# Bias rows of a routed expert layer, made in the routing stage of one core's kernel

## The chip, the cores and the metric

The kernel runs on one core of one Trainium2 chip as a single program. The metric is device time in microseconds (us), taken as the median of several executions; lower is better. Engines are called PE (TensorE), DVE (VectorE), ACT (ScalarE), POOL (GpSimd) and SP (SyncE, which here only starts transfers).

## The reference

One layer of an encoder with 16 meta tokens and 1024 tokens of width 1024, all in fp32. What matters here is what follows attention:

```python
mixed = jnp.concatenate([out_a, out_b], axis=-1)
h = h + mixed @ w_out[l]
v = _rmsnorm(h, g_ffn[l]).reshape(B * L, D_MODEL)
y = _moe(v, ...)          # logits = v @ w_router + b_router; top 4 of 32 experts; gates = softmax(top 4)
h = h + y.reshape(B, L, D_MODEL)
...
def expert_block(args):
    xb, e = args
    a = xb @ w_mlp1[e] + b_mlp1[e]
    return _clamped_swiglu(a) @ w_mlp2[e] + b_mlp2[e]
ys = ys * slot_gate[:, None].astype(ys.dtype)
return jax.ops.segment_sum(ys, slot_tok, num_segments=T + 1)[:T]
```

The part with `b_mlp2` can be split off: for each token it is the sum over its four experts of gate times `b_mlp2[e]`, that is one row of `gates (1024 x 32) @ b_mlp2 (32 x 1024)`. These are the "bias rows".

## The kernel before, in words

**Stages.** Five stages follow one another: `project`, `attend_window`, `attend_diff`, `route`, `experts`. Each is a block: every engine has its own instruction list, engines wait for one another only through semaphores, and a block ends when all five have arrived. An engine's list is worked through strictly in order, so an instruction that waits holds up all behind it on its engine. The change touches `route` and `experts` only.

**fp32 products.** A product is made of fp32r parts: a "high" copy (ACT) and a "low" remainder (DVE: value minus high), and three matmuls, high x high, high x low, low x high.

**`route`** handles eight tiles of 128 tokens (`NT` = 8), in a software pipeline. In PE's iteration t it does: `project_out(t, 0)` (24 matmuls of 512 columns), `transpose_mixed(t + 1)`, `ranks(t - 2)`, `transpose_v(t - 1, 0)`, half of `project_out(t, 1)`, `transpose_v(t - 1, 1)`, the other half, `logits(t - 1)`. DVE's iteration t does: `residual(t, 0)`, `copy_mt(t + 1)` (the low parts of the turned tile), `place(t - 2)` (gates, slot numbers, and a dense row of gates per token, L1359), `heads(t + 2)`, `residual(t, 1)`, `normalise(t)`, in iteration 4 the low part of `b_mlp2` (L1383), `choose(t - 1)` (top 4, ends with `sel`, L1342). ACT makes high parts, squares, roots and exponents. SP stores each tile of h (`sums`, the output tensor) and of v (`v_dram`). POOL scatters each token's number and gate to its four slots in `slot_dram` (L1223, an indirect DMA per pick) and at the stage's end waits until all 32 scatters have landed. After the last tile DVE and PE make the list of jobs (L1387 to L1416): a job is up to 256 slots of one expert; the kinds are "one" (up to 128), "few" (up to 192) and "two".

**`experts`** first sets up, then runs a loop over the jobs. Setting up before the change:

- SP reads the first job's slots (`idn`, L1621), then starts loading weights; each weight piece is 1 MB, twelve to a job, and four pieces of the first expert were loaded during `route`.
- POOL clears `xg`, gathers the first job's rows of v (L1652), spreads `b_mlp1` over the partitions (L1667), and adds the bias rows to the output tensor by eight accumulating DMAs (L1670).
- PE turns the dense gates (L2111), makes the bias rows in eight steps of two matmuls (L2119), each step waiting until ACT or DVE has emptied the bank of the step before last, then turns the first job's rows (`transpose_x0(0)`, L1996), waits for the last copies and enters the job loop.
- ACT makes the high part of the gates (L1819), the high parts of weight pieces 0 to 2 (L1732), four copies of bias rows (L1824), `keep_x0(0)` (L1757), and enters the loop.
- DVE makes the low part of the gates (L1973), the low parts of pieces 0 to 2 (L1845), four copies (L1979), `keep_x0(0)` (L1904), waits until the first three accumulating DMAs have landed, and enters the loop.

In the loop PE's first product needs the low part of the first rows (`x0_lo`) and of piece 0; piece k + 3 is split in step k of the loop.

Of the kernel before, what the change touches and what calls it, by code (L numbers as in the profile page):

```python
# [26 lines left out]
P = 128  # L27
D = 1024
# [512 lines left out]
class BiasRows:  # L541
# [3 lines left out]
    HIGH, LOW = slice(N_EXP, 2 * N_EXP), slice(2 * N_EXP, 3 * N_EXP)  # L545

    def __init__(self, nc, ctx):
        sb = lambda n, s, d=F32: ctx.enter_context(nc.sbuf_tensor(n, s, d))
        self.ident = sb("ident5", [P, P])
        self.dense = sb("dense_gates", [P, NT, 3, N_EXP])  # L550
        self.b2_p = sb("b2_parts", [3 * N_EXP, D], F32R)
# [560 lines left out]
def route(nc, a, mixed, gates, picks, jobs, bias, sums, v_dram, slot_dram, weights):  # L1112


    with ExitStack() as ctx:
# [13 lines left out]
        h2 = sb("h2", [P, 2, D])  # L1129
# [21 lines left out]
        b2 = sb("b2", [3 * N_EXP, D])  # L1151
        share = sb("share", [P, TOP_K, N_EXP])
# [4 lines left out]
        h2_sem = [sem(f"h2_stored{i}") for i in range(2)]  # L1157
# [12 lines left out]
        b2_landed, b2_high = sem("b2_landed"), sem("b2_high")  # L1170
# [10 lines left out]
        turned = lambda: tm_ps[:, :, :].rearrange("p b (c n) -> p (b c) n", n=P)  # L1181

        @block.sync
        def _(sp):
# [8 lines left out]
            sp.dma_start(bias.ident[:, :], a["consts"][:, C_ID:C_ID + P]).then_inc(b2_landed, 16)  # L1193
            for t in range(NT):
                sp.wait_ge(h2_done, 2 * (t + 1))
                sp.dma_start(sums[t * P:(t + 1) * P, :], h2[:, t % 2, :]).then_inc(h2_sem[t % 2], 16)
# [8 lines left out]
            for i in range(2):  # L1205
                sp.wait_ge(h2_sem[i], 16 * (NT // 2))
                sp.wait_ge(v_sem[i], 16 * (NT // 2))

        @block.gpsimd
        def _(pool):  # L1210

            pool.memset(none[:, :, 1], 0).then_inc(ready, 1)
# [13 lines left out]
            pool.wait_ge(scattered, 16 * NT * TOP_K)  # L1226

        @block.scalar
        def _(act):
# [15 lines left out]

            act.wait_ge(landed, 16 * NL)
# [7 lines left out]
            for t in range(NT + 1):  # L1254
                if t + 1 < NT:
                    copy_mt(t + 1)
                if t >= 1:
                    u = t - 1
                    for b in range(2):
                        act.wait_ge(tv_ready, 2 * u + b + 1)  # L1260
                        if b == 0 and u >= 1:
                            act.wait_ge(r_ready, u)
                        act.copy(vt[:, 4 * b:4 * b + 4, :], tv_ps[:, :].rearrange("p (c n) -> p c n", n=P)).then_inc(vt_done, 1)
                if t + 2 < NT:
                    head_std(t + 2)
                if t < NT:
# [4 lines left out]
                    act.activation(vs[:, t % 2, :], h2[:, t % 2, :], ACT.Square, accum_out=ss[:, t:t + 1]).then_inc(ss_done, 1)  # L1271
                    act.wait_ge(ss_done, t + 1)
                    act.activation(rs[:, t:t + 1], ss[:, t:t + 1], ACT.Sqrt, bias=eps[:, 0:1], scale=1.0 / D).then_inc(std_done, 1)
                if t == 3:
                    act.wait_ge(b2_landed, 64)
                    act.copy(bias.b2_p[:, :], b2[:, :]).then_inc(b2_high, 1)
                if t >= 1:
# [5 lines left out]
        def _(dve):  # L1283
# [31 lines left out]
            def residual(t, b):  # L1315
                dve.wait_ge(x_sem[t % 2], 16 * (t // 2 + 1))
                if t >= 2:
                    dve.wait_ge(v_done, t - 1)
                    dve.wait_ge(h2_sem[t % 2], 16 * (t // 2))
                dve.wait_ge(o_ready, 2 * t + b + 1)  # L1320
                dve.tensor_tensor(h2[:, t % 2, 512 * b:512 * b + 512], o_ps[:, 2 * (t % 2) + b, :],
                                  xs[:, t % 2, 512 * b:512 * b + 512], ALU.add).then_inc(h2_done, 1)

            def normalise(t):
                dve.wait_ge(std_done, t + 1)
                step(dve.reciprocal(rs[:, t:t + 1], rs[:, t:t + 1]))
                dve.scalar_tensor_tensor(out=vs[:, t % 2, :], in0=h2[:, t % 2, :], scalar=rs[:, t:t + 1], in1=gf[:, :],
# [16 lines left out]
            def place(u):  # L1344
# [7 lines left out]
                for k in range(TOP_K):  # L1352
# [6 lines left out]
                step(dve.tensor_reduce(bias.dense[:, u, :, :], share[:, :, :].rearrange("p k e -> p e k").unsqueeze(1)  # L1359
                                       .broadcast_to((P, 3, N_EXP, TOP_K)), AX.X, ALU.add))  # L1360
# [8 lines left out]
            for t in range(NT + 2):  # L1369
                if t < NT:  # L1370
                    residual(t, 0)
                if t + 1 < NT:
                    copy_mt(t + 1)
                if t >= 2:
# [6 lines left out]
                if t == 4:  # L1381
# [827 lines left out]
```

## Time and profile before

| | us |
|---|---|
| median of 3 runs | 2428.54 (2428.15 to 2431.27) |
| the profiled execution's own time | 2426.24 |
| its span, first to last instruction | 2424.6 |
| of it, `route` | 726.2 to 890.0 |
| first matmul of the job loop | 916.8 |
| last matmul of the job loop | 2408.0 |
| PE busy, share of the span | 2281.5 (94%) |

All times of rows are from the profiled execution, from the start of its span. The mean granted clock of PE over it is 0.971 of full speed. A row of the timeline has start, duration, engine, line, operation and tiles; in brackets stand the idle time before it and what ended it.

### The profile page before, as it was taken

How to read it: one execution, taken by the hardware profiler on the slowest of the kernel's cores; microseconds unless marked ns; L12 is line 12 of the kernel's file. 1: busy time of each engine (PE TensorE's matmuls, PEld its weight loads, DVE VectorE, ACT ScalarE, POOL GpSimd, SP SyncE). 2: the span in 40 equal slices, each digit the busy share in tenths (PEclk: the TensorE clock that was granted, in tenths of full speed). 3: DMA queues.
4: the chain of work that ended last, by engine and by line, in shares of the span. 5: the costliest groups of instructions: out<-in, count | busy, mean ns of one | idle time of the engine just before them, and what ended most of it. 6: DMA issues, size and time to landing. Idle time of an engine off the chain costs nothing. (4 is left out here: it accounts for less than half of the span.)

```text
span 2424.6 us, 34957 instructions
## 1 busy us (share of the span) xinstructions
PE 2281.5 (94%) x10657; PEld 1715.7 (71%) x10658; DVE 1874.5 (77%) x2403; ACT 1399.9 (58%) x1672; POOL 593.9 (24%) x555
## 2 busy tenths in 40 slices
PE   6999699999998948999999999999999999999996
PEld 5778565555546836777777877777777777777875
DVE  4476455999966757889897589788888878989986
ACT  4322354888864436666675457565656555757755
POOL 0133000111110233324142113231133221423523
PEclk9999799899998958999999999999999999999999
DMA  5243730333105639889797669796889777979986
GB/s 161 64 122 97 154 65 22 99 71 70 36 1 158 106 123 317 319 285 341 268 371 243 200 234 362 275 319 224 268 288 313 241 236 245 370 245 364 376 293 225
DMA packets 251919, 519.68 MB, mean 214 GB/s; under 512 B 28657, under 2 KB 60657, under 8 KB 251809
## 3 DMA queue, kind: packets, MB, share of 16 engines
q1 hardware_dynamic: 229666, 480.01, 58.8%
q0 software_dynamic: 22176, 38.70, 7.0%
q8 instruction: 42, 0.69, 0.1%
q14 instruction: 35, 0.29, 0.0%
HBM read 493.06 MB, written 60.15 MB: 228 GB/s over the span
## 5 line engine op out<-in xcount | busy, mean ns | idle before, releaser
L1845 DVE TENSOR_TENSOR wlo<-raw_first,whi 128x2048 fp32r<-128x2048 f32 x259 | 618.6, 2406 | 115.4 <-ACT whi L1732 103.2
L1732 ACT CAST whi<-raw_first 128x2048 fp32r<-128x2048 f32 x259 | 489.3, 1907 | 144.4 <-PE gl_ps L2024 95.0
L2026 PE MATMUL gl_ps<-whi,xt_hi 128*128 128x512 f32 x1056 | 418.6, 396 | 16.2 <-DVE wlo L1845 7.8
L2028 PE MATMUL gl_ps<-whi,xt_lo 128*128 128x512 f32 x1056 | 412.4, 391 | 0.0
L2027 PE MATMUL gl_ps<-wlo,xt_hi 128*128 128x512 f32 x1056 | 412.2, 390 | 0.0
L1845 DVE TENSOR_TENSOR wlo<-raw_later,whi 128x2048 fp32r<-128x2048 f32 x128 | 292.1, 2282 | 57.2 <-ACT whi L1732 57.2
L1732 ACT CAST whi<-raw_later 128x2048 fp32r<-128x2048 f32 x128 | 240.9, 1908 | 65.7 <-PE gl_ps L2024 48.0
L2026 PEld LDWEIGHTS gl_ps<-whi,xt_hi 128*128 128x128 f32 x1056 | 198.7, 188 | 69.3 <-issue 11.9
L2028 PEld LDWEIGHTS gl_ps<-whi,xt_lo 128*128 128x128 f32 x1056 | 198.8, 188 | 42.9
L2027 PEld LDWEIGHTS gl_ps<-wlo,xt_hi 128*128 128x128 f32 x1056 | 199.0, 188 | 40.0
L1652 POOL DMA_INDIRECT xg<-v_dram,idn x67 | 123.4, 1841 | 402.6 <-PE t_ps L1996 318.4
L2026 PE MATMUL y_ps<-whi,ht_hi 128*128 128x512 f32 x512 | 206.5, 403 | 0.0
L2028 PE MATMUL y_ps<-whi,ht_lo 128*128 128x512 f32 x512 | 200.0, 391 | 0.0
L2027 PE MATMUL y_ps<-wlo,ht_hi 128*128 128x512 f32 x512 | 199.5, 390 | 0.0
L757 DVE CUSTOM_DVE_ANT_0 e<-s_ps,zero,meta_nm 128x1024 f32<-128x1024 f32 x128 | 163.5, 1278 | 11.7 <-DVE dsb L772 9.6
L2024 PE MATMUL gl_ps<-wlo,xt_hi 128*64 128x512 f32 x416 | 164.7, 396 | 0.0
L2023 PE MATMUL gl_ps<-whi,xt_hi 128*128 128x512 f32 x416 | 162.3, 390 | 0.0
L1705 POOL DMA_INDIRECT out_h<-ys,idc x64 | 126.8, 1981 | 122.1 <-ACT ys L1776 76.7
L685 ACT ACTIVATE e<-e,nm 128x1040 f32<-128x1040 f32 x128 | 149.1, 1165 | 9.5 <-DVE nm L757 8.4
L870 PE MATMUL o_ps<-pt,v_all 128*64 128x512 f32 (+1 forms) x288 | 139.0, 605 | 0.0
L484 PE MATMUL pp<-w_in_hi,ut_hi 128*128 128x512 f32 (+3 forms) x344 | 132.0, 384 | 2.4 <-DVE ut_lo L345 2.4
L1701 POOL PARTITION_BROADCAST b<-b x32 | 91.9, 2873 | 166.7 <-DMA b<-in_b_mlp 163.6
(282 smaller groups left out, 4045.4 us busy)
## 6 DMA issues: line engine op xcount, KB each, us to landing
raw_first<-in_w_mlp SPq DMA_DIRECT2D x260, 1024.0 KB
raw_later<-in_w_mlp SPq DMA_DIRECT2D x130, 1024.0 KB
k_st<-qk_dram SPq DMA_DIRECT2D x32, 260.0 KB, 7.4
xs<-in_x SPq DMA_DIRECT2D x16, 512.0 KB, 3.9
w_in_raw<-in_w_in SPq DMA_DIRECT2D x32, 256.0 KB
q_st<-qk_dram SPq DMA_DIRECT2D x32, 256.0 KB, 6.6
qk_dram<-qk_hi SPq DMA_DIRECT2D x24, 256.0 KB, 2.4
qk_dram<-qk_lo SPq DMA_DIRECT2D x24, 256.0 KB, 2.8
```

The source lines that it names most:

```text
L484: pe.matmul(out, ut_hi[:, k, cols(i)], whi[:, s, 0:w], start=(k == 0), stop=False)
L685: act.activation(e[:, n % 2, i, :], e[:, n % 2, i, :], ACT.Exp, bias=nm[:, k:k + 1], scale=-1.0, accum_out=total[:, n % 16, i:i + 1]).then ...
L757: dve.tensor_tensor_reduce(e[:, n % 2, i, 0:SEQ], S(i), zero[:, :], -1.0, meta_nm[:, (n // NT) % 2, at:at + 1], ALU.add, ALU.min, nm[:, k: ...
L870: ins = pe.matmul(o_ps[DV:P, :], vt, pt[0:r, g % 2, c, :], start=(c == 0), stop=(c == 8), skip_group_check=True)
L1705: pool.indirect_dma_start(out=sums[:, :], out_offset=bass.IndirectOffsetOnAxis(ap=idc[:, half, 0:1], axis=0), in_=ys[:, half, :], in_offse ...
L1732: act.copy(whi[:, k % SPL, :], raw(k)).then_inc(hi_done, 1)
L1845: dve.tensor_tensor(wlo[:, k % SPL, :], raw(k), whi[:, k % SPL, :].bitcast(F32), ALU.subtract).then_inc(lo_done, 1)
L2023: ins = pe.matmul(bank, xh[:, 1, kc, :], hi, start=start, stop=stop, skip_group_check=True)
L2024: ins = pe.matmul(bank[0:FEW], xh[:, 1, kc, 0:FEW], lo, start=False, stop=stop, skip_group_check=True)
L2026: pe.matmul(bank, xh[:, half, kc, :], hi, start=start, stop=False, skip_group_check=True)
L2027: pe.matmul(bank, xh[:, half, kc, :], lo, start=False, stop=False, skip_group_check=True)
L2028: return pe.matmul(bank, xl[:, half, kc, :], hi, start=False, stop=stop, skip_group_check=True)
```

## The change

- `BiasRows` becomes `FirstRows`, which holds the buffers of the first job's rows (`xg`, `idn`), one more tile of sums (`last`) and three semaphores, so that they live through both stages.
- In `route`, h of tile t is kept in SBUF: in `mixed[:, t, :]`, whose attention output has been used by then, and for the last tile in `last`. DVE's `residual` no longer waits for earlier stores of h.
- Each tile's gates are turned on PE (`turn_gates`), split by ACT (`high_gates`) and DVE (`low_gates`), multiplied on PE (`bias_row`, two matmuls of 512 columns) into banks that the stage already has, and added by DVE (`add_row`) to the kept h. SP stores the sum only then (`store_sum`). The low part of `b_mlp2` is made in DVE's iteration 3, before 4.
- At the end of `route` SP waits for the scatters and reads the first job's slots, and POOL gathers the first job's rows there; POOL clears `xg` at the stage's start.
- On PE the last two calls, `turn_gates(NT - 1)` and `bias_row(NT - 1)`, stand among and behind the matmuls of the job list. From `experts` all work on bias rows is gone: the turning of the gates, eight products, eight copies, eight accumulating DMAs and the waits for them. POOL clears `ys` at its start.

```diff
 (DVE, place)
-                step(dve.tensor_reduce(bias.dense[:, u, :, :], ..., AX.X, ALU.add))
+                if u >= 2:
+                    dve.wait_ge(gt_ready, u - 1)
+                dve.tensor_reduce(dense[:, u % 2, :, :], ..., AX.X, ALU.add).then_inc(dense_done, 1)
+            def low_gates(u):
+                dve.wait_ge(gt_high, u + 1)
+                dve.tensor_tensor(gates_p[HIGH, u % 2, :], gt_ps[HIGH, :], gates_p[HIGH, u % 2, :].bitcast(F32), ALU.subtract
+                                  ).then_inc(gt_low, 1)
+            def add_row(u):
+                dve.wait_ge(row_ready, u + 1)
+                dve.wait_ge(v_done, u + 1)
+                dve.tensor_tensor(h2(u).rearrange("p (b n) -> p b n", n=512), row_bank(u),
+                                  h2(u).rearrange("p (b n) -> p b n", n=512), ALU.add).then_inc(row_added, 1)
...
             for t in range(NT + 2):
+                if 3 <= t <= NT:
+                    low_gates(t - 3)
+                if 4 <= t <= NT - 1:
+                    add_row(t - 4)
                 if t < NT:
                     residual(t, 0)
...
+                if t == NT + 1:
+                    low_gates(NT - 2)
                 if t >= 2:
                     place(t - 2)
...
                     residual(t, 1)
                     normalise(t)
-                if t == 4:
+                if t == 3:
                     dve.wait_ge(b2_high, 1)
+                    dve.tensor_tensor(b2_p[LOW], b2[LOW, :], b2_p[LOW].bitcast(F32), ALU.subtract).then_inc(b2_low, 1)
+                if t == NT:
+                    add_row(NT - 4)
+                    add_row(NT - 3)
                 if 1 <= t <= NT:
                     choose(t - 1)
 (DVE, behind the job list)
+            add_row(NT - 2)
+            add_row(NT - 1)
 (PE, transpose_mixed)
                 if t >= 1:
                     pe.wait_ge(mt_low, t)
+                if t >= 5:
+                    pe.wait_ge(row_added, t - 4)
 (PE)
+            def turn_gates(u):
+                pe.wait_ge(dense_done, u + 1)
+                pe.wait_ge(vt_done, 2 * min(u + 2, NT - 1))
+                if u >= 1:
+                    pe.wait_ge(gt_low, u)
+                pe.transpose(gt_ps, dense[:, u % 2, :, :].rearrange("p i e -> p (i e)"), ident).then_inc(gt_ready, 1)
+            def bias_row(u):
+                pe.wait_ge(gt_low, u + 1)
+                if u == 0:
+                    pe.wait_ge(b2_low, 1)
...
+                for c in range(2):
+                    ins = pe.matmul(row_bank(u)[:, c, :], gates_p[:, u % 2, :], b2_p[:, 512 * c:512 * c + 512], start=True, stop=True)
+                ins.then_inc(row_ready, 1)
...
+                project_out(t, 1, KC // 2, KC)
+                if t >= 3:
+                    bias_row(t - 3)
+                if t >= 1:
                     logits(t - 1)
+                if t >= 2:
+                    turn_gates(t - 2)
+            transpose_v(NT - 1, 0)
+            transpose_v(NT - 1, 1)
+            ranks(NT - 2)
+            bias_row(NT - 3)
+            logits(NT - 1)
+            turn_gates(NT - 2)
+            ranks(NT - 1)
+            bias_row(NT - 2)
...
 (SP)
+            def store_sum(u):
+                sp.wait_ge(row_added, u + 1)
+                sp.dma_start(sums[u * P:(u + 1) * P, :], h2(u)).then_inc(sums_stored if u < NT - 1 else rows1.last_stored, 16)
...
+            for u in range(NT - 4, NT - 1):
+                store_sum(u)
+            sp.wait_ge(scattered, 16 * NT * TOP_K)
+            sp.dma_start(rows1.idn[:, :, :], slot_dram[0:JOB, :]...).then_inc(idx_first, 16)
+            store_sum(NT - 1)
+            sp.wait_ge(sums_stored, 16 * (NT - 1))
 (POOL)
-            pool.wait_ge(scattered, 16 * NT * TOP_K)
+            for i in range(2):
+                pool.wait_ge(v_sem[i], 16 * (NT // 2))
+            pool.wait_ge(rows_set, 1)
+            pool.wait_ge(idx_first, 16)
+            for half in range(2):
+                pool.indirect_dma_start(out=rows1.xg[:, half, :], ..., in_=v_dram[:, :], ...).then_inc(rows1.x_landed[half], 16)
 (experts, PE)
-            for t in range(NT):
-                ins = pe.transpose(t_ps[...], bias.dense[:, t, :, :]..., ident[:, :])
-            ins.then_inc(gt_ready, 1)
-            pe.wait_ge(gt_low, 1)
-            for t in range(NT):
-                if t >= 2:
-                    pe.wait_ge(b_copied[t % 2], t // 2)
-                for c in range(2):
-                    ins = pe.matmul(bias_banks(t)[:, c, :], gates_p[:, t * P:(t + 1) * P], bias.b2_p[...], start=True, stop=True)
-                ins.then_inc(b_ready, 1)
             transpose_x0(0)
-            for half in range(2):
-                pe.wait_ge(b_copied[half], NT // 2)
 (experts, DVE)
-            for t in range(1, NT, 2):
-                dve.wait_ge(b_ready, t + 1)
-                dve.tensor_copy(stage[t], bias_banks(t)).then_inc(b_copied[1], 1)
             keep_x0(0)
-            dve.wait_ge(b_stored[0], 16 * 3)
```

## Rows read from the trace of the kernel before

**Rows 1.** The page, busy time of PE.
```profile
PE 2281.5 (94%) x10657; PEld 1715.7 (71%) x10658; DVE 1874.5 (77%) x2403; ACT 1399.9 (58%) x1672; POOL 593.9 (24%) x555
```
**Rows 2.** Windows: engines' busy time, then clock, DMA share, GB/s.
```profile
798.67:813.65 14.98, 14.98 (x87) 12.86 (x86) 11.56 (x38) 7.64 (x12) 4.19 (x4) 1.00 0.88 106
...
859.40:864.90 5.50, 0.01 (x1) 0.01 (x1) 3.36 (x14) 3.45 (x7) 0.00 (x0) 0.58 0.50 184
...
889.96:916.81 26.85, 12.29 (x32) 7.65 (x33) 14.04 (x9) 12.68 (x11) 13.38 (x12) 0.50 0.93 276
```
**Rows 3.** Timeline of PE in `route`, iterations 4 and 5.
```profile
804.25 1.03 PE L1429 MATMUL tm_ps<-cst,mixed 128*128 128x128 f32 x8
...
811.95 1.86 PE L1461 MATMUL r_ps<-w_router_sb,vt 128*128 128x32 f32 x16
...
821.36 0.41 PE L1467 MATMUL r_ps<-acc,ones 128*128 128x32 f32 x2 [1.10 <-DVE sel L1342]
```
**Rows 4.** Timeline of DVE in `route`, iterations 3 and 4.
```profile
801.64 1.28 DVE L1327 SCALAR_TENSOR_TENSOR vs<-h,rs,g_ffn_sb 128x1024 f32<-128x1024 f32 x1
...
806.37 1.22 DVE L1307 TENSOR_TENSOR mt_lo<-tm_ps,mt_hi 128x1024 fp32r<-128x1024 f32 x1 [0.81 <-ACT mt_hi L1240]
...
817.94 1.22 DVE L1383 TENSOR_TENSOR b_parts<-b,b_parts 32x1024 fp32r<-32x1024 f32 x1
...
820.93 0.37 DVE L1342 TENSOR_REDUCE sel<-chosen 128x32 f32<-128x128 f32 x1
```
**Rows 5.** Timeline of the end of `route`.
```profile
867.84 0.82 DVE L1359 TENSOR_REDUCE dense_gates<-share 128x96 f32<-128x384 f32 x1
...
869.38 3.62 PE L1461 MATMUL r_ps<-w_router_sb,vt 128*128 128x32 f32 x16 [0.68 <-ACT vt L1263]
...
873.12 0.19 DVE L1333 TENSOR_TENSOR lg<-r_ps,b_router_sb 128x32 f32<-128x32 f32 x1 [4.45 <-issue]
...
882.07 0.96 POOL L1223 DMA_INDIRECT slot_dram<-code,dsti  x1 [0.30 <-issue]
...
885.33 0.15 DVE L1416 CAST jobs<-r_ps 1x1 int32<-1x1 f32 x1
```
**Rows 6.** POOL's sequencer at the block's end: ns, start in us.
```profile
L1115 POOLq COMPARE_BRANCH  x1: 49/49/49, 886.8 to 886.8; - x1
L1115 POOLq DRAIN  x1: 2758/2758/2758, 886.9 to 886.9; - x1
```
**Rows 7.** Timeline of the start of `experts`.
```profile
889.96 0.38 SPq L1621 DMA_DIRECT2D idn<-slot_dram  x1
...
892.81 1.06 POOL L1652 DMA_INDIRECT xg<-v_dram,idn  x1 [1.03 <-DMA idn<-slot_dram]
...
894.18 1.01 POOL L1652 DMA_INDIRECT xg<-v_dram,idn  x1 [0.30 <-issue]
...
895.54 6.70 DVE L1845 TENSOR_TENSOR wlo<-raw_first,whi 128x2048 fp32r<-128x2048 f32 x3 [0.58 <-ACT whi L1732]
...
904.05 2.30 POOL L1667 PARTITION_BROADCAST b<-b  x1 [8.86 <-issue]
...
912.64 1.23 DVE L1904 TENSOR_TENSOR xt_lo<-t_ps,xt_hi 128x1024 fp32r<-128x1024 f32 x1 [1.53 <-ACT xt_hi L1757]
...
916.81 0.79 PE L2026 MATMUL gl_ps<-whi,xt_hi 128*128 128x512 f32 x1 [5.26 <-PEq L2070]
```
**Rows 8.** DMA issues, 745 to 960: KB each, median us to landing.
```profile
out_h<-h SPq DMA_DIRECT2D x8, 512.0 KB, 5.1
...
xg<-v_dram,idn POOLq DMA_INDIRECT x5, 7.6
```
**Rows 9.** Timeline between the first job and the second.
```profile
957.50 0.49 PE L2026 MATMUL gl_ps<-whi,xt_hi 128*128 128x512 f32 x1 [3.63 <-DVE wlo L1845]
...
957.71 2.30 POOL L1701 PARTITION_BROADCAST b<-b  x1
...
957.88 4.13 DVE L1845 TENSOR_TENSOR wlo<-raw_first,whi 128x2048 fp32r<-128x2048 f32 x1 [1.12 <-ACT whi L1732]
```

More of the change, by code:

```diff
@@ L1108, in _, with route @@
                     act.copy(ot[:, u % 2, :], o_ps[0:DV, :]).then_inc(ot_done, 1)
-def route(nc, a, mixed, gates, picks, jobs, bias, sums, v_dram, slot_dram, weights):
+def route(nc, a, mixed, gates, picks, jobs, rows1, sums, v_dram, slot_dram, weights):
     with ExitStack() as ctx:
@@ L1128, in route @@
         mt_lo = sb("mt_lo", [P, 2, KC, P], F32R)
-        h2 = sb("h2", [P, 2, D])
         vs = sb("vs", [P, 2, D])
@@ L1253, in _ @@
             head_std(1)
-            for t in range(NT + 1):
+            for t in range(NT + 3):
+                if 3 <= t:
+                    high_gates(t - 3)
                 if t + 1 < NT:
                     copy_mt(t + 1)
-                if t >= 1:
+                if 1 <= t <= NT:
                     u = t - 1
@@ L1497, in _, with experts @@
             pe.matmul(r_ps[0:1, 128 + 2 * NJ:128 + 3 * NJ], ec[:, 2:3], ej[:, 2, :], start=True, stop=True).then_inc(cnt_ready, 1)
-def experts(nc, a, first, bias, jobs, v_dram, slot_dram, sums):
+            bias_row(NT - 1)
+def experts(nc, a, first, rows1, jobs, v_dram, slot_dram, sums):
     with ExitStack() as ctx:
@@ L1527, in experts @@
         b1 = sb("b1", [P, 2 * D])
-        idn = sb("idn", [P, 2, 2], U32)
+        idn = rows1.idn
         idm = sb("idm", [P, 2, 2], U32)
         idc = sb("idc", [P, 2, 2], U32)
-        ident = bias.ident
-        rows = sb("bias_rows", [P, OWN, 2, 512])
-        ys_parts = lambda half: ys[:, half, :].rearrange("p (c n) -> p c n", n=512)
-        stage = [sg[:, :, :], lin[:, :, :], hh[:, :, :], ys_parts(0), ys_parts(1), *[rows[:, i, :, :] for i in range(OWN)]]
+        ident = rows1.ident
         gl_ps = ps("gl_ps", [P, 2, 2, 512])
@@ L2148, in build @@
                 attend_diff(nc, a, v_all, mixed, qk_dram, stacks, weights)
-            bias = BiasRows(nc, whole)
-            route(nc, a, mixed, gates, picks, jobs, bias, sums, v_dram, slot_dram, weights)
-        experts(nc, a, first, bias, jobs, v_dram, slot_dram, sums)
+            rows1 = FirstRows(nc, whole)
+            route(nc, a, mixed, gates, picks, jobs, rows1, sums, v_dram, slot_dram, weights)
+        experts(nc, a, first, rows1, jobs, v_dram, slot_dram, sums)
 def rope_table():
```

142 lines of the change are left out of this document (69 added, 73 removed).

## The prediction

> **What bounds the kernel now.** I read the page first: PE is busy 94% of the span [rows 1], so time can be won only where PE isn't. The waits of PE after the first job are small, so the job loop moves as a whole with its start, and the start is all that this change can move. The windows then show three places. In `route` a tile costs 14.98 us in which PE never rests [rows 2]. At the stage's end PE does almost nothing. And from 889.96, the start of `experts`, to 916.81, the first product of the job loop, 26.85 us pass with PE busy for 12.29, at half clock (0.50) [rows 2].
>
> The timeline tells that DVE is nearly as full as PE in `route`. PE's iteration 4 starts at 798.67; it turns the next tile at 804.25 and reaches `logits` at 811.95 [rows 3]. DVE keeps just ahead: in iteration 5, which starts at 813.65, `ranks` waits 1.10 us for DVE's `sel` [rows 3], because the low part of `b_mlp2` (1.22 us) stood before it on DVE [rows 4]. So DVE has almost no room, and the change gives both engines more to do there.
>
> **Part 1, `route`, tile 3: a new wait.** `bias_row(0)` is on PE between `project_out(3, 1)` and `logits(2)`, and waits for `b2_low`. DVE makes that in iteration 3 behind `residual(3, 1)` and `normalise(3)`, which need that very projection. In the row `normalise(3)` ends at 801.64 + 1.28 = 802.92 [rows 4]; the low part adds 1.2, so 804.1. PE arrives at 811.95 - 14.98 = 796.97 [rows 2, 3], plus 0.2 for `turn_gates(0)`. PE waits 804.1 - 797.2 = 6.9 us, and behind it stand `logits(2)`, for which DVE's `choose(2)` waits, and the next projection. After an idle stretch of 5.5 us the granted clock had fallen (0.58 over it) and `logits` took 3.62 us where it takes 1.86 at full clock [rows 2, 3, 5]; after one of 3.63 us a 512-column matmul still took 0.49 [rows 9]. 6.9 is beyond both, so I count the slow clock: 1.8 on `logits`, 0.4 on two matmuls. Sum 6.9 + 2.2 = **+9.1** (bounds: 6.5 with the clock kept, 10).
>
> **Part 2, `route`, more work.** A matmul of 512 columns costs (804.25 - 798.67) / 24 = 0.23 us [rows 2, 3]. Before the last residual stand four bias rows (8 x 0.23) and five turnings of gates, one small transpose each, which I put at 0.2 from the 1.03 / 8 of the transposes [rows 3] plus a restart: 1.9 + 1.0 = **+2.9** (2 to 4).
>
> **Part 3, `route`, DVE against PE.** From tile 5 on, `transpose_mixed(t + 1)` waits for `add_row(t - 4)`. On DVE that stands behind `choose` and `low_gates`. No row shows `add_row`; `copy_mt` has its shape and a PSUM input: 1.22 us [rows 4]. `low_gates` is small: 0.2. DVE's round is then: turning to `copy_mt` 806.37 - 804.25 = 2.1 [rows 3, 4]; from there to the end of `sel`, at 821.30, 14.9, less the 1.2 that leaves iteration 4, 13.7 [rows 4]; `low_gates` and `add_row` 1.5. Sum 17.3, against PE's 14.98 + 0.67 = 15.6. PE waits 1.7 us per tile in iterations 5 and 6 (in 4 DVE has caught up during the wait of part 1, in 7 nothing is turned): +3.4. The waits of before go: the iteration from 813.65 took 1.4 more than 14.98, and 0.3 in the last. **+1.7** (-1 to +5). The sum up to the last `residual` is +13.7. The stores of h moved on SP wait for nothing late there. ACT's `high_gates` and the moved copy of `b_mlp2` fall in gaps of ACT (7.64 busy of 14.98) [rows 2]; without that cover 0.3 a tile.
>
> **Part 4, the end of `route`.** Times here are those of before; all come 13.7 later. PE now turns tile 7 in two spare banks without waiting for ACT between, so its clock is more likely kept. `choose(7)` started at 873.12 when `logits(7)` at half clock was done [rows 5]. After, `logits` waits for the slots of tile 6, ready at 867.4; DVE then makes the dense gates (0.82, from 867.84 [rows 5]) and two `add_row`s and is ready at 870.8, behind which `logits` (1.86) hides. Everything behind is 2.3 earlier: the job list ends at 885.48 - 2.3 = 883.2 [rows 5]. Now what closes the block. Before, POOL's last scatter was issued by 883.03 and had landed at 886.8; a drain of 2.76 followed, and the block opened at 889.96, 3.2 after the wait [rows 5, 6, 7]. After, SP is the one queue for three things: `store_sum(6)` waits for `add_row(6)`, the last but one instruction of DVE, at 883.2 + 1.2 = 884.4; the slots' read comes behind it at 884.8 (the scatters, 2.3 earlier, have landed at 884.5). Issue of that read to the first gather was 892.81 - 889.96 = 2.85, first gather to the end of the second 2.38 [rows 7]. POOL is free at 884.8 + 2.85 + 2.38 = 890.0; with the same drain the block opens at 893.2. SP waits for row 6's store, 884.4 + 5.1 [rows 8] = 889.5, DVE ends at 885.7: both earlier. **+3.2** (bounds: 0.9 with no drain; +7, if the drain lasts until the gathers, 7.6 us each [rows 8], have landed).
>
> **Part 5, the start of `experts`.** Let B be the block's opening. Removed from PE's path: turning the gates, the gates' parts, and eight products paced by copies. POOL's slots read and gathers are done before. What is left before PE's first product: ACT's table load and three high parts; DVE's three low parts, which started 1.92 after ACT's first, in the rows 6.70 us for the three [rows 7]. ACT can start at B + 1.3, so DVE splits from B + 3.2 to B + 9.9, and `keep_x0` (1.23 [rows 7]) ends at B + 11.2. PE's own queue: the gathered rows land at 887.7 + 7.6 = 895.3 [rows 8], B + 2.1; eight turnings at half clock 1.9; and 5.3 us of sequencer, seen before the first product [rows 7]: B + 9.3, hidden behind DVE. PE starts at B + 11.2 instead of B + 26.85: **-15.65** (-17 to -11.5). DVE enters its loop no later after PE than before, so the first job doesn't stretch; weights aren't late, for piece 9 is requested earlier relative to its use and the accumulating DMAs, 4 MB with their share of a full DMA window (0.93) [rows 2], are gone.
>
> The first job's `b_mlp1` was spread at 904.05, B + 14.1 [rows 7], after DVE's splits. Between jobs 1 and 2 such a broadcast at 957.71 ran beside a split, which took 4.13 us for 2.23 [rows 7, 9]. The Trainium skill, "SBUF — State Buffer", section "SBUF: two separate sides", says that a VectorE operation with two SBUF inputs and a GpSimd operation that reads SBUF exclude one another; the row agrees (4.13 us). If the bias lands some 4 us sooner with the queues emptier, the third split would wait by that rule, and the sum would be 1.9 higher. I take the row's place for it, behind the splits, and nothing.
>
> **Sum.** 9.1 + 2.9 + 1.7 + 3.2 - 15.65 = +1.25 us. The profiled execution took 2426.24 with a span of 2424.6; after, 2425.9 and 2427.5. The runs' median is 2.3 above the profiled one, and I forecast it by the same difference: 2428.54 + 1.25 = 2429.8.
>
> **Rivals.**
>
> *The drain waits for the gathers* (slower). The drain row, 2.76 us, stood behind scatters that had landed [rows 6]. If it holds the block until the second gather lands, that is 889.0 + 7.6 = 896.6, B = 897.0, 3.8 later. Against it: the drain didn't scale with anything outstanding there. It decides from +3.6 on. Total +5.1: 2433.6. Chance 0.15.
>
> *The start gives back less* (slower). Each engine's first read of the job list and its code stand in series before the loop; if these fall after `keep_x0` and not beside it, B + 11.2 becomes B + 15 to B + 16. For: PE had 5.26 us of it [rows 7]. Against: PE's queue has nothing before it but the turning. Total about +5.5: 2434. Chance 0.12.
>
> *PE doesn't wait in tile 3* (faster). If DVE's low part of `b_mlp2` is ready when PE comes, part 1 falls away: 1.25 - 9.1 = -7.85, 2420.7; the change would do what it removes. Against it the order on DVE and the rows of part 1. For it only what I may misread, or a lighter part 3. Chance 0.18.
>
> *As summed*: 0.55.
>
> **Numbers.** A difference under 0.2% (4.9 us) can't be told from none. The forecast case lies within that for 0.47 of its 0.55, 0.04 on either side; the drain case is close to the bound: 0.05 within, 0.10 slower; the start case slower 0.12; the last faster 0.18. So faster 0.22, same 0.52, slower 0.26. The range leaves out the far halves of the outer cases: 2421 to 2435; the forecast's own is 2425 to 2434.
>
> **What would show it.** Part 1: one wait of PE of about 7 us, `bias_row(0)` on the low part of `b_mlp2`, then matmuls at twice their time. Part 3: PE waiting for `add_row` before turning tiles 6 and 7, some 1.7 us each. Part 4: POOL's gathers behind the slots' read, itself behind a store, then a drain; the block opening some 17 us later than before. Part 5: 11 us from there to the first product, DVE's `keep_x0` the last releaser. The prediction is wrong if the first wait is missing, if the opening comes 20 us later, or if these 11 us are 15.

## The result, and the profile after

| | before | after |
|---|---|---|
| median, us | 2428.11 (14 runs) | 2432.41 (14 runs) |
| ratio of the changed kernel to the one before | | 1.002 (95%: 1.0012 to 1.0027) |
| profiled execution: own time, span | 2426.24, 2424.6 | 2430.15, 2428.5 |
| `route` ends, `experts` opens | 890.0 | 909.5 |
| first product of the job loop | 916.81 | 920.73 |

The change costs 4.3 us on the medians, 0.2%. The interval of the ratio lies wholly above 1, so the loss is small but clear of the scatter. (One of the 14 executions of the changed kernel took 5349.5 us, for a reason that the record does not show, and is in no ratio.) In the profiled executions the losses are where the sum had them. PE is as busy as before, in the same number of matmuls:

```profile
PE 2280.6 (94%) x10657; PEld 1715.3 (71%) x10658; DVE 1882.3 (78%) x2414; ACT 1396.3 (57%) x1675; POOL 593.4 (24%) x549
```

The windows show iterations 4, 5 and 6 of `route` and then the start of `experts` up to the first product (columns as in [rows 2]):

```profile
808.29:825.10 16.81, 16.81 (x89) 14.31 (x89) 11.09 (x37) 4.12 (x8) 3.21 (x4) 0.91 0.08 27
825.10:842.40 17.30, 15.66 (x91) 13.23 (x90) 12.97 (x41) 6.85 (x12) 4.06 (x5) 1.00 0.47 92
842.40:859.70 17.30, 15.62 (x91) 13.21 (x90) 10.82 (x36) 6.46 (x13) 4.06 (x5) 1.00 0.41 93
909.54:920.73 11.19, 1.94 (x8) 1.57 (x9) 7.96 (x5) 9.49 (x6) 2.20 (x3) 0.50 0.74 247
```

An iteration took 14.98 us before [rows 2]; now it takes 16.8 to 17.3. In the first of the three PE never rests, but part of it ran at half clock (granted clock 0.91 over it); in the last two PE rests 1.6 to 1.7 us. The start of `experts` took 26.85 us [rows 2] and takes 11.19. The timeline of PE in `route` tells what it waits for:

```profile
803.95 1.19 PE L1557 MATMUL tm_ps<-b_parts,gates_parts 96*128 96x512 f32 x2 [7.05 <-issue]
804.94 3.46 PE L1530 MATMUL r_ps<-w_router_sb,vt 128*128 128x32 f32 x16
...
808.29 0.77 PE L1506 MATMUL o_ps<-w_out_hi,mt_hi 128*128 128x512 f32 x1
808.86 0.63 PE L1507 MATMUL o_ps<-w_out_lo,mt_hi 128*128 128x512 f32 x1
809.29 0.63 PE L1508 MATMUL o_ps<-w_out_hi,mt_lo 128*128 128x512 f32 x1
...
832.50 1.06 PE L1494 MATMUL tm_ps<-cst,mixed 128*128 128x128 f32 x8 [1.64 <-DVE mixed L1410]
...
849.80 1.06 PE L1494 MATMUL tm_ps<-cst,mixed 128*128 128x128 f32 x8 [1.68 <-DVE mixed L1410]
...
877.38 1.97 PE L1522 MATMUL o_ps<-cst,vs 128*128 128x128 f32 x8 [2.87 <-DVE vs L1365]
...
882.28 3.59 PE L1530 MATMUL r_ps<-w_router_sb,vt 128*128 128x32 f32 x16 [0.80 <-DVE dsti L1394]
```

Before the first bias row (L1557) PE stands idle for 7.05 us. Behind that wait the sixteen matmuls of `logits` take 3.46 us where they took 1.86 [rows 3], and the next projection's matmuls start 0.43 us apart instead of 0.23. At 832.50 and 849.80 PE waits for `add_row` (L1410). In the last rows, the end of the stage, the transposes and `logits(7)` run at half clock once more. The timeline of DVE:

```profile
802.63 1.22 DVE L1440 TENSOR_TENSOR b_parts<-b,b_parts 32x1024 fp32r<-32x1024 f32 x1
...
830.81 0.28 DVE L1404 TENSOR_TENSOR gates_parts<-tv_ps,gates_parts 32x128 fp32r<-32x128 f32 x1
831.13 1.22 DVE L1410 TENSOR_TENSOR mixed<-tm_ps,mixed 128x1024 f32<-128x1024 f32 x1
...
872.33 0.69 DVE L1359 TENSOR_TENSOR last_sum<-o_ps,xs 128x512 f32<-128x512 f32 x1 [2.15 <-PE o_ps L1508]
...
898.27 0.15 DVE L1477 CAST jobs<-r_ps 1x1 int32<-1x1 f32 x1
```

The low part of `b_mlp2` (L1440) ends at 803.85, and PE's wait ends at 803.95. `low_gates` takes 0.28 us and `add_row` 1.22. The last `residual(7, 0)` starts at 872.33, 14.5 us later than its row in the kernel before (timeline of DVE there):

```profile
857.82 0.69 DVE L1321 TENSOR_TENSOR h<-o_ps,xs 128x512 f32<-128x512 f32 x1 [3.10 <-PE o_ps L1443]
```

The end of the stage, in the order of the three queues (scatter, slots' read, gathers):

```profile
895.09 0.96 POOL L1249 DMA_INDIRECT slot_dram<-code,dsti  x1 [0.30 <-issue]
...
900.09 0.43 SPq L1230 DMA_DIRECT2D idn<-slot_dram  x1
...
903.50 1.05 POOL L1257 DMA_INDIRECT xg<-v_dram,idn  x1 [7.45 <-DMA idn<-slot_dram]
904.86 1.01 POOL L1257 DMA_INDIRECT xg<-v_dram,idn  x1 [0.30 <-issue]
```

and POOL's sequencer at the block's end (columns as in [rows 6]):

```profile
L1117 POOLq DRAIN  x1: 5459/5459/5459, 903.8 to 903.8; - x1
```

The last scatter is issued 13 us later than in [rows 5], the slots are read at 900.09, the gathers are issued at 903.50 and 904.86, and the DRAIN, entered at 903.8, ends at 909.3. The block opens at 909.54. The start of `experts`, answering to [rows 7], with the spreading of `b_mlp1` and the fourth split beside it:

```profile
912.77 6.70 DVE L1918 TENSOR_TENSOR wlo<-raw_first,whi 128x2048 fp32r<-128x2048 f32 x3 [11.96 <-ACT whi L1810]
919.38 1.22 DVE L1977 TENSOR_TENSOR xt_lo<-t_ps,xt_hi 128x1024 fp32r<-128x1024 f32 x1
...
920.37 2.30 POOL L1752 PARTITION_BROADCAST b<-b  x1 [8.98 <-issue]
920.52 4.16 DVE L1918 TENSOR_TENSOR wlo<-raw_first,whi 128x2048 fp32r<-128x2048 f32 x1
...
920.73 0.79 PE L2092 MATMUL gl_ps<-whi,xt_hi 128*128 128x512 f32 x1 [8.46 <-DVE xt_lo L1977]
```

The three splits, `keep_x0` and the first product follow one another without a gap. The product waits for `xt_lo` alone.

### The profile page after: what moved, and what is told of

Its sections match the earlier page's. It is cut to its first block and busy times, and to the rows that moved or that the text cites. A ratio compares the mean times of both kernels' runs of the same rounds, so it can differ in the third digit from the quotient of the medians.

```text
span 2428.5 us, 34980 instructions
## 1 busy us (share of the span) xinstructions
PE 2280.6 (94%) x10657; PEld 1715.3 (71%) x10658; DVE 1882.3 (78%) x2414; ACT 1396.3 (57%) x1675; POOL 593.4 (24%) x549
## 5 line engine op out<-in xcount | busy, mean ns | idle before, releaser
L1740 POOL DMA_INDIRECT xg<-v_dram,idn x65 | 116.5, 1792 | 404.9 <-PE t_ps L2062 330.5
```

## The experiments

The runs of a round were timed beside the kernel before on one chip; between the rounds its medians agree within 1.1 us. The profiled executions differ by up to 4.4 us in the time at which they reach the same point of `route`, so the table counts the first product of the job loop from one fixed row, the start of `logits` in `route`'s third iteration (767.03 in the kernel before), and shows its shift against the kernel before's 149.78 us.

| run | first product, shift | median, us | before, us | ratio (95%) |
|---|---|---|---|---|
| the change | +4.15 | 2432.41 | 2428.11 | 1.0020 (1.0012 to 1.0027) |
| e1_low_part_early | -4.57 | 2423.62 | 2428.49 | 0.9979 (0.9970 to 0.9988) |
| e2_gathers_back | +3.21 | 2430.49 | 2428.49 | 1.0012 (1.0003 to 1.0021) |
| e3_before_no_rows | -10.40 | 2429.03 | 2428.49 | 1.0007 (0.9998 to 1.0016) |
| e4_thin_sums | +3.15 | 2431.51 | 2428.49 | 1.0011 (1.0002 to 1.0020) |
| e5_no_rows_code_kept | -12.44 | 2416.38 | 2428.39 | 0.9949 (0.9935 to 0.9963) |
| e6_before_gathers_early | +6.56 | 2436.35 | 2428.39 | 1.0034 (1.0022 to 1.0046) |
| z1_slots_early_gathers_late | -1.70 | 2427.51 | 2428.39 | 0.9999 (0.9990 to 1.0008) |
| z2_both_mended | -10.23 | 2416.77 | 2428.39 | 0.9951 (0.9938 to 0.9965) |
| z3_first_rows_before_splits | -11.43 | 2417.69 | 2429.22 | 0.9950 (0.9937 to 0.9964) |
| z2_again | -10.87 | 2416.55 | 2429.22 | 0.9954 (0.9940 to 0.9967) |

The shift of the first product and the shift of the median agree within 2 us in every run but one, e3. So the claim that the job loop moves as a whole with its start holds to some 2 us, and e3 needs a cause of its own. The single profiled executions are looser: from its first to its last product the loop took 1490.8 us in the kernel before, 1491.2 in the changed one, 1491.7 to 1495.8 in the other runs, and 1504.5 in e3.

### e1_low_part_early: the wait in tile 3

```diff
@@ ACT
-                if t == 2:
+                if t == 0:
                     act.wait_ge(b2_landed, 64)
                     act.copy(b2_p[:, :], b2[:, :]).then_inc(b2_high, 1)
@@ DVE
-                if t == 3:
+                if t == 0:
                     dve.wait_ge(b2_high, 1)
```

> The changed kernel with one edit: the high and low part of b_mlp2 are made in iteration 0 of the stage and not in 2 and 3. Theory of the sum: the 7 us for which PE waits in tile 3 and its two slow microseconds behind go (9.1), but DVE no longer catches up there, so PE waits for add_row in iteration 4 as well (+1.7): 7.4 us less than the changed kernel, 2425, that is some 3 us under the kernel before. Rival, DVE paces the stage anyway and the wait only moves: within 2 us of the changed kernel, 2431 to 2433.

Timeline of PE, `logits` of iteration 3 and the waits behind it:

```profile
799.53 1.87 PE L1530 MATMUL r_ps<-w_router_sb,vt 128*128 128x32 f32 x16
...
808.69 1.06 PE L1494 MATMUL tm_ps<-cst,mixed 128*128 128x128 f32 x8 [1.68 <-DVE mixed L1410]
...
826.00 1.07 PE L1494 MATMUL tm_ps<-cst,mixed 128*128 128x128 f32 x8 [1.68 <-DVE mixed L1410]
...
843.30 1.06 PE L1494 MATMUL tm_ps<-cst,mixed 128*128 128x128 f32 x8 [1.65 <-DVE mixed L1410]
```

The 7 us wait is gone, `logits` takes 1.87 us again, and the run is 8.8 us below the changed kernel. There are now three waits for `add_row`, not two: without the pause in tile 3 DVE has nothing to catch up in, and the wait begins one iteration sooner. This alone makes the change a gain.

### e2_gathers_back: the gathers on the other side of the block's end

```diff
@@ route, SP
-            sp.dma_start(rows1.idn[:, :, :], slot_dram[0:JOB, :]...).then_inc(idx_first, 16)
@@ route, POOL
-            pool.wait_ge(idx_first, 16)
-            for half in range(2):
-                pool.indirect_dma_start(out=rows1.xg[:, half, :], ...)
+            pool.wait_ge(scattered, 16 * NT * TOP_K)
@@ experts, SP and POOL
+            sp.dma_start(idn[:, :, :], slot_dram[0:JOB, :]...).then_inc(idx_first, 16)
+            pool.wait_ge(idx_first, 16)
+            for half in range(2):
+                gather(half)
```

> The changed kernel with the slots' read and the two gathers of the first job back at the start of experts; the bias rows stay in route. Theory: at the end of route they cost more than they save, since the drain behind them took 5.46 us and not 2.76, and slots' read and gathers stand in series before it. The block opens at 903.1 instead of 909.5, the first product comes 15 us later, at 918: 2.6 us less than the changed kernel, 2430. Rival, the drain is 5 us whatever stands before it and the early gathers save their 4 us: 3 to 4 us more than the changed kernel, 2436.

POOL's sequencer at the block's end, and the timeline of PE behind it:

```profile
L1117 POOLq DRAIN  x1: 2762/2762/2762, 900.5 to 900.5; - x1
```

```profile
915.01 1.97 PE L2061 MATMUL t_ps<-ident,xg 128*128 128x128 f32 x8 [19.05 <-DMA xg<-v_dram,idn]
919.41 0.79 PE L2091 MATMUL gl_ps<-whi,xt_hi 128*128 128x512 f32 x1 [2.44 <-DVE xt_lo L1976]
```

The DRAIN is short again and the next block opens at 903.56, 5.6 us before the changed kernel's when both are counted from the fixed row. Now the gathered rows are late: PE turns them at 915.01, and the first product comes at 919.41, 0.9 us earlier by the table. The median is 1.9 us lower, which the two intervals do not separate. So each place of the gathers has a price: at the end of `route` they hold the block, at the start of `experts` PE waits for them.

### e3_before_no_rows and e5_no_rows_code_kept: what the bias rows cost at the start

e3 is the kernel before without its bias rows; its output lacks the `b_mlp2` term. POOL clears `ys` in their place.

```diff
@@ experts, PE (the copies, the accumulating DMAs and their waits are left out likewise)
-            for t in range(NT):
-                ins = pe.transpose(t_ps[...], bias.dense[:, t, :, :]..., ident[:, :])
-            ins.then_inc(gt_ready, 1)
-            pe.wait_ge(gt_low, 1)
-            for t in range(NT):
-                ...
-                for c in range(2):
-                    ins = pe.matmul(bias_banks(t)[:, c, :], ...)
-                ins.then_inc(b_ready, 1)
             transpose_x0(0)
-            for half in range(2):
-                pe.wait_ge(b_copied[half], NT // 2)
```

> The kernel before with all work on bias rows left out of experts (no turning of the gates, no products, copies and accumulating DMAs); the output lacks the b_mlp2 term. It shows what the start of experts can give back at most while the gathers stay there. Theory: the first product waits for the gathered rows and comes at the opening + 15.0 instead of + 26.85: 11.8 us less than the kernel before, 2416.3. Rival, the start is paced by the sequencers and the weights: 5 us less or under, 2423.

The first product came 10.4 us earlier against the fixed row, and the time did not move. That was neither theory's number. The gain is lost in one place, 470 us later, between two jobs (timeline of PE):

```profile
1373.40 0.39 PE L2010 MATMUL gl_ps<-whi,ht_lo 128*128 128x512 f32 x1
1382.83 0.79 PE L2008 MATMUL gl_ps<-whi,xt_hi 128*128 128x512 f32 x1 [9.04 <-issue]
1383.42 0.63 PE L2009 MATMUL gl_ps<-wlo,xt_hi 128*128 128x512 f32 x1
```

PE stands still for 9.04 us, and the profile names nobody ("issue"). DVE's last split ahead of that product had ended at 1372.62. What the trace has in that stretch is traffic on the queue of instructions, 1350 to 1400 (packets, MB, share):

```profile
q8 instruction: 6, 0.10, 1.0%
```

Two of the six lie inside PE's idle time. In the kernel before one packet stands in the 50 us, and PE is busy for all of them. From 930 us to the end e3 has 16 packets on that queue and every other run 10. So I took the idle time for a fetch of code, brought on because 24 instructions were missing ahead of the loop and all of PE's loop lay elsewhere. e5 puts 24 small transposes in their place:

```diff
@@ experts, PE, on top of e3
+            for t in range(NT):
+                pe.transpose(t_ps[0:3 * N_EXP, 0, 0:P], bias.dense[:, t, :, :]..., ident[:, :])
+                for c in range(2):
+                    pe.transpose(t_ps[0:3 * N_EXP, 1, 0:P], bias.dense[:, t, :, :]..., ident[:, :])
             transpose_x0(0)
```

> The kernel before without its bias rows again (its output lacks the b_mlp2 term), as in the run e3_before_no_rows, but with 24 small transposes of 96 x 128 in TensorE's stream where the 24 left-out products and turns stood, so that all of TensorE's code behind them lies where it lay before. Nobody waits for their results, and TensorE waits for the first rows at that place anyway. In the run without rows the job loop's first product came 12.4 us earlier against the same point of the kernel before, but TensorE then idled 9.04 us near 1374 with nothing in front of it that the profile shows (issue), and the instruction queue moved 6 packets in 1350 to 1400 where the kernel before moved 1. Theory: that idle time is a fetch of code, which came about because the loop's code was moved, not a price of an earlier start. Then with the code where it was the idle time and the 6 packets are gone, and of the 12.4 us some 10 are left at the end (2 go to the clock, which fell to half at job 1 in that run): 2428.5 - 10 = 2418.5 us. Rival: the loop cannot give an earlier start to the end, because weights or scattered stores run as they did: then the idle time comes back at the same or another place and the time is 2427 to 2430.

The queue of instructions in the same stretch, 1350 to 1400:

```profile
q8 instruction: 1, 0.02, 0.1%
```

The idle time is gone, with it the extra packets, and the median is 2416.38 us: 12.65 below e3. The parts add up to about that: the wait 9.0, the matmuls at half clock behind it about 2.0 (ten, 0.43 us apart instead of 0.23), and an earlier start 2.0. The bias rows are worth 12 us in the kernel before by the medians; in the profiled execution the loop gives 2.4 us of them back (1493.1 us for 1490.8). Shown is that the idle time came with the 24 missing instructions and not with the missing work on bias rows. That it is a fetch of code is inferred from the instruction queue alone. The added transposes also moved the start by 2.0 us, so another effect of timing is not excluded, and why it came at just that place stays open.

### e4_thin_sums: is it DVE's addition that PE waits for

The bias rows of tiles 0 to 3 are added in 8 of 512 columns a bank, so most of that term is missing from them.

```diff
@@ DVE, add_row
-                dve.tensor_tensor(h2(u)..., row_bank(u), h2(u)..., ALU.add)
+                w = 512 if u >= 4 else 8
+                dve.tensor_tensor(h2(u)...[:, :, 0:w], row_bank(u)[:, :, 0:w], h2(u)...[:, :, 0:w], ALU.add)
```

> The changed kernel with add_row of tiles 0 to 3 cut from 1024 to 16 columns; the other columns of these tiles lack their bias term. It takes 1.1 us from DVE's round and nothing from PE. Theory: DVE paces iterations 5 and 6 with 1.64 and 1.68 us of PE's wait, so each is 1.1 shorter: 2.2 us less than the changed kernel, 2430.2. Rival, PE's waits there are not DVE's length but the order of the semaphores: no change.

Timeline of PE in `route`, the two waits for the addition:

```profile
834.94 1.06 PE L1495 MATMUL tm_ps<-cst,mixed 128*128 128x128 f32 x8 [0.61 <-DVE mixed L1411]
...
851.19 1.06 PE L1495 MATMUL tm_ps<-cst,mixed 128*128 128x128 f32 x8 [0.60 <-DVE mixed L1411]
```

The two waits fall from 1.64 and 1.68 to 0.61 and 0.60. The first product comes only 1.0 us earlier: in iteration 4 of this execution twelve matmuls behind the 7.05 us wait ran at half clock and not seven, so PE came to the first of the two waits 1.1 us later. What shows DVE's pace is the time between the two turnings, in which the clock was full: 16.25 us for 17.30. So DVE is the pace there, as said, and the addition is 1.05 us of it. The median is 0.9 lower, which is no more than the scatter.

### e6_before_gathers_early: the other part of the change alone

The kernel before with the slots' read and the gathers at the end of `route`; the bias rows stay.

```diff
@@ route, SP
+            sp.wait_ge(scattered, 16 * NT * TOP_K)
+            sp.dma_start(bias.idn[:, :, :], slot_dram[0:JOB, :]...).then_inc(bias.idx_first, 16)
@@ route, POOL
-            pool.wait_ge(scattered, 16 * NT * TOP_K)
+            pool.wait_ge(bias.free, 1)
+            pool.memset(bias.xg[:, :, :], 0.0).then_inc(bias.set, 1)
+            ...
+            pool.wait_ge(bias.idx_first, 16)
+            for half in range(2):
+                pool.indirect_dma_start(out=bias.xg[:, half, :], ...)
```

> The kernel before with one part of the change alone: the first job's slots are read and its rows gathered at the end of the route stage, the bias rows stay in the experts' block. (The 96 rows of b_mlp2 lie in the gathered rows' buffer until they are split, so that the buffer fits; GpSimd clears it after the last scatter.) Theory: the gathers and what stands behind them hold the end of the block. In the kernel before the last scatter was issued at 882.07 and the next block opened at 889.96, with a DRAIN of 2.76 us on GpSimd; in the changed kernel the DRAIN behind the gathers took 5.46 us, and the block opened 5.6 us later than in the run with the gathers moved back. So the block opens 5.5 to 7 us later, near 896, and nothing is given back, because the first product waits for the bias rows, 26.85 us behind the block's opening, and not for the gathered rows: 2428.5 + 6 = 2434.5 us. Rival: the gathers are what the start of the experts waits for; then the first product comes less than 26.85 us behind the opening and the time is 2429 or below.

POOL's sequencer at the block's end, then the timeline of the second gather and of the first product:

```profile
L1120 POOLq DRAIN  x1: 5442/5442/5442, 888.9 to 888.9; - x1
```

```profile
889.94 1.01 POOL L1240 DMA_INDIRECT xg<-v_dram,idn  x1 [0.30 <-issue]
...
921.11 0.79 PE L2035 MATMUL gl_ps<-whi,xt_hi 128*128 128x512 f32 x1 [2.92 <-DVE xt_lo L1913]
```

8.0 us slower. The DRAIN is 5.44 us again, here with no bias row in `route`, and ends 3.4 us after the second gather's work on POOL is over (889.94 + 1.01); in the changed kernel it is 3.4 as well (904.86 + 1.01 to 909.3). So 2.0 of the 5.4 us pass before the second gather's work is over, since the DRAIN's row begins ahead of that gather, and the price of gathers before a block's end is the slots' wait, the gathers and 3.4 us behind them.

### z1, z2, z3: mends

z1 is the changed kernel with the slots read on SP at the end of `route` and the gathers at the start of `experts`.

```diff
@@ route, POOL
-            pool.wait_ge(idx_first, 16)
-            for half in range(2):
-                pool.indirect_dma_start(out=rows1.xg[:, half, :], ...)
+            pool.wait_ge(scattered, 16 * NT * TOP_K)
@@ experts, POOL
+            pool.wait_ge(rows1.idx_first, 16)
+            for half in range(2):
+                gather(half)
```

> The changed kernel with the two halves of its early loads parted: the slots are still read on the queue of SP at the end of the route stage, behind the last scatter, while the two gathers are again the first thing that GpSimd does in the experts' block. Theory: a DRAIN behind gathers costs 5.46 us against 2.76, and the wait for the slots adds the rest of the 5.6 us by which the block opens later; with the slots read beside the DRAIN the block opens near 904, the gathers are issued at once and land near 909.5, the turned rows are there when VectorE is through its three splits (913.4), and the first product comes 11 us behind the opening, near 915 (changed kernel: 920.73): 5 to 6 us less than the changed kernel, 2426.5 to 2427.5 us. Rival: what counts is when the gathered rows land, and that is not earlier than in the changed kernel by more than 1 to 2 us, as in the run with slots and gathers moved back: 2430 to 2431 us.

The sequencers of POOL and SP at the block's end, then the timeline of the start of `experts`:

```profile
L1118 POOLq DRAIN  x1: 2762/2762/2762, 900.6 to 900.6; - x1
...
L1118 SPq DRAIN  x1: 7/7/7, 902.5 to 902.5; - x1
```

```profile
904.40 1.05 POOL L1737 DMA_INDIRECT xg<-v_dram,idn  x1 [8.42 <-POOLq L1118]
...
909.28 1.97 PE L2062 MATMUL t_ps<-ident,xg 128*128 128x128 f32 x8 [13.05 <-DMA xg<-v_dram,idn]
914.79 0.79 PE L2092 MATMUL gl_ps<-whi,xt_hi 128*128 128x512 f32 x1 [3.54 <-DVE xt_lo L1977]
```

The read of the slots runs beside POOL's DRAIN, the gathers are issued at 904.40, and the rows are turned while DVE is still splitting. The first product comes 5.9 us before the changed kernel's and the median is 4.9 lower, where 5 to 6 were expected. SP waits for the last stores of sums until 902.5, and POOL's DRAIN, which ends at 903.3, is still the last to arrive.

z2 is z1 with the edit of e1.

> The two mends together: the low part of b_mlp2 is made at the start of the route stage (as in the run e1_low_part_early, 2423.6 us, 8.8 us below the changed kernel), and the slots are read early while the gathers are issued in the experts' block (as in the run z1 of this call). Theory: the two lie at different places of one chain (the first before the last residual, the second behind the last scatter) and add: 2423.6 - 5.5 = 2418 us, below both kernels. Rival: the second part gives only 1 to 2 us: 2422 us.

Measured 2416.77, and 2416.55 in the second measurement: 0.9951 and 0.9954 of the kernel before. The two gains add: -8.8 and -4.9 from 2432.4 give 2418.7, and the measured medians are 2 us below that. It beats both kernels.

The two profiled executions of this one kernel also show what the clock does to it. In both PE waits 1.68 us for `add_row` in iteration 4. Behind the wait seven matmuls ran at half clock in the one and none in the other (windows, z2_both_mended, then z2_again; columns as in [rows 2]):

```profile
808.50:811.00 2.50, 2.50 (x8) 2.01 (x7) 2.04 (x7) 0.88 (x2) 0.00 (x0) 0.50 0.49 166
```

```profile
807.50:810.00 2.50, 2.50 (x13) 2.05 (x12) 1.98 (x6) 0.84 (x2) 0.00 (x0) 1.00 0.55 180
```

> The kernel of the run z2_both_mended unchanged, for a second measurement of it beside z3 on the same chip: 2416.8 us, 11 to 12 us below the kernel before.

z3 is z2 with the first rows' split ahead of the second and third piece of weights.

```diff
@@ ACT and DVE
-            for k in range(AHEAD):
-                split(0, k)
+            split(0, 0)
             keep_x0(0)
+            for k in range(1, AHEAD):
+                split(0, k)
```

> The kernel of the run z2_both_mended with one thing more: ScalarE and VectorE split the first block of weights, then the first job's turned rows, and only then the second and third block (as it stands all three blocks come first). In that run TensorE had turned the rows at 903.1, VectorE was in its three splits until 905.4, wrote xt_lo until 906.5, and the first product came at 906.68. Theory: with the rows ahead of blocks two and three, xt_hi is there at 904.1 and xt_lo at 905.3, so the first product comes 1.3 us earlier, and the late splits are covered by the products of the first block (12 matmuls of 0.43 us and the second half's turns): 2415.5 us. Rival: the two late splits come after TensorE wants them, and the start is as late as before or later: 2417 to 2419 us.

Timeline of PE, the first job's first products, then the second job's first:

```profile
905.26 0.79 PE L2094 MATMUL gl_ps<-whi,xt_hi 128*128 128x512 f32 x1 [2.44 <-DVE xt_lo L1978]
...
910.12 0.56 PE L2096 MATMUL gl_ps<-whi,xt_lo 128*128 128x512 f32 x1
```

```profile
947.70 0.54 PE L2094 MATMUL gl_ps<-whi,xt_hi 128*128 128x512 f32 x1 [4.93 <-ACT whi L1810]
```

The first product comes 0.6 to 1.2 us earlier against the fixed row than in the two measurements of z2, as the theory had it, and the time is 1.1 us higher: a miss for it, within the scatter. From first product to second job's first product z3 takes 42.4 us, z2_again 41.4. The rows show 0.7 of that 1.1: the matmuls ran 0.43 us apart and not 0.23 for the first 4.9 us (z2_again: 4.0), that is two more of them at half clock; and the second job waits 4.93 us for the high part of its weights (z2_again: 4.63).

## Why the prediction was right, and where its terms were off

Forecast was 2429.8, with a range of 2421 to 2435, that is +1.3; measured was 2432.41, that is +4.3. Every step is in the trace, in its place. The mechanism was right. The sum was too good in four stretches, by 0.8 us up to the last `residual`, 0.7 in the tail, 1.1 at the block's opening and 0.5 in the loop, so it forecast less than a third of the loss.

**Part 1 (+9.1).** Right. The wait is 7.05 us for 6.9, its releaser the low part of `b_mlp2`, though the profile writes "issue" for it; that it is this one is shown by e1, in which it is gone and 8.8 us with it. Iteration 4 starts 9.6 us later than before. The slow clock was mis-sized: I had 1.8 on `logits` and 0.4 on two matmuls. `logits` lost 1.6, the two matmuls 0.5, and seven matmuls of the next projection, which the sum had at full clock, another 1.4: 3.5 for 2.2.

**Part 2 (+2.9) and part 3 (+1.7).** Right in kind. A turning of gates costs PE some 0.05 us and not 0.2: from `logits` to the next projection it is 1.75 us (823.37 to 825.12) where it was 1.70 (811.95 to 813.65). Five of them are 0.8 less than the sum had. `low_gates` 0.28 and `add_row` 1.22 were put at 0.2 and 1.22; the iterations were to take 17.3 us and took 17.30 and 17.30; the waits were to be 1.7 and were 1.64 and 1.68. Up to the last `residual` the sum was +13.7, measured +14.5: the 0.8 is what is left of the slow clock (1.3 more) and a slightly longer wait, less the cheaper turnings.

**Part 4 (-2.3, then the block 10.0 us behind the job list).** The tail gave only -1.6. Its forecast had the clock kept; PE waited 2.87 us at 877.38, the transposes and `logits(7)` ran at half clock (3.59 us), and so `logits` and not DVE's additions set `choose(7)`. By its own rows the sum should have let the additions end at 867.84 + 0.82 + 2 x 1.22 = 871.1 and not at 870.8; the three operations overlapped a little and took 3.06 us (882.36 to 885.42), so that slip cost nothing. From the end of the job list (898.42) the block took 11.1 us to open: read of the slots +1.7 (1.6 forecast), to the first gather 3.4 (2.85), the gathers 2.4 (2.4), to the opening 3.7 (3.2). The order on SP and POOL was right; 1.1 us is spread over its terms. The block opened 19.6 us later than before, where 17 was forecast and 20 was to be a sign of being wrong; the 2.6 are the 0.8 from before the last `residual`, the 0.7 of the tail and this 1.1. The DRAIN row did double, 2.76 to 5.46. The rival that let it wait for the landing of the gathers had the price wrong (+3.8, from a landing of 7.6 us), but its mechanism is not excluded. The DRAIN ends 3.4 us after POOL's work on the second gather in the changed kernel and in e6; it also ends 1.5 us after that gather has landed in both, since the landing took 2.9 us from its issue in the one and in the other. No run separates the two readings. If it does wait for the landing, the forecast's 3.2 was near the measured 3.7 by luck, since the landing was so much quicker than the 7.6 us of [rows 8].

**Part 5 (-15.65).** Measured 11.19 for 26.85: -15.66. The chain was the forecast one, three splits on DVE (6.70), `keep_x0` (1.22), product. `b_mlp1` was spread from 920.37 for 2.30 us, behind the three splits, and the fourth split next to it took 4.16 us instead of 2.23. The Trainium skill, "SBUF — State Buffer", section "SBUF: two separate sides", would have two such operations exclude one another, and the row agrees (4.16 us). PE did not wait for it: from 920.73 to 950 its rows show no wait.

**Sum.** 14.5 - 1.6 + 6.6 - 15.7 = +3.9 at the first product, where 13.7 - 2.3 + 5.5 - 15.65 = +1.25 was forecast. Behind it the loop adds 0.5: after a wait of 3.01 us between the first and the second job, matmuls ran 0.43 us apart for 3 us (timeline of PE in the changed kernel), where in the kernel before, after 3.63 us [rows 9], they didn't.

```profile
960.19 0.49 PE L2092 MATMUL gl_ps<-whi,xt_hi 128*128 128x512 f32 x1 [3.01 <-DVE wlo L1918]
...
961.83 0.63 PE L2092 MATMUL gl_ps<-whi,xt_hi 128*128 128x512 f32 x1
962.26 0.63 PE L2093 MATMUL gl_ps<-wlo,xt_hi 128*128 128x512 f32 x1
```

**Rivals.** "PE doesn't wait in tile 3" was false of this kernel and is true of e1, at 2423.6 where 2420.7 was its number; what it left out is the third wait for `add_row` (1.7) and the end of the stage (0.7 and 1.1 short), against which the turnings were 0.8 cheaper. "The start gives back less" was false.

## What to carry to other kernels

A computation moved from an idle start into a busy pipeline is paid by its first use there: a 1.2 us preparation put three iterations earlier, where nobody waits for it, was worth twice the whole loss of this change. Gathers pulled across a block's end held the block here until 3.4 us after POOL's work on the last of them; split such a chain, so that the short read lies beside the end and the long one behind it. And where an edit at one place shows its gain in the trace but not in the time, look for one idle stretch that names nobody before giving up the mechanism.

## What the runs showed of the hardware

- PE idled 9.04 us between two jobs in a kernel from which 24 earlier PE instructions had been taken, with 6 packets on the instruction queue in 50 us for 1 (e3); with 24 small instructions in their place it didn't idle and the time was 12.65 us lower (e5).
- The row of POOL's DRAIN at a block's end was 2.76 us behind landed scatters (kernel before, e2, z1, z2) and 5.44 to 5.46 with two gathers at its start (the changed kernel, e1, e6). It then ended 3.4 us after POOL's work on the second gather and 1.5 us after its landing.
- The granted clock of PE is not read off the length of one wait: after 3.63 us it was kept (0.23 us a matmul, the 2.4 GHz level), after 3.01 us in the changed kernel it fell to half (0.43 us) 1.2 us after work had begun again. Behind a wait of 1.68 us it fell to half in one execution of z2's kernel (granted clock 0.50) and stayed full in the other (1.00). So which matmuls run at half clock differs between two executions of one kernel, here by seven matmuls or 1.4 us.
